# The prompt's up projection as seven half-size products (Strassen), with the sample's tokens as a plain pass in front

## The reference, cut to what matters

```
h = rmsnorm(x, norm2_g)
u = dwconv3(h @ w_up, ffn_conv_w, ffn_conv_b)     # w_up: 1024 x 5632; neighbours along the tokens
val, gate = u[..., :D_FF], u[..., D_FF:]           # D_FF = 2816
return x + (jax.nn.silu(gate) * val) @ w_down      # w_down: 2816 x 1024
```

## Time and profile before

| | |
|---|---|
| median of the runs | 2340.96 us (2334.17 to 2341.86) |
| span of the profiled execution | 2335.3 us |
| busy: PE, DVE, ACT, POOL | 2240.7, 1184.1, 782.4, 145.3 us |
| up projection, first to last matmul's start | 1238.3 to 1958.5 us |

### The profile page before, as it was taken

How to read it: one execution, slowest core, us unless ns; L and a number is a source line. 1 busy time by engine, 2 the same in 40 slices (tenths; PEclk the granted TensorE clock), 3 DMA queues, 4 the chain that set the end, 5 groups by cost and what they waited for, 6 DMA issues and landing times.

```text
span 2335.3 us, 26185 instructions
## 1 busy us (share of the span) xinstructions
PE 2240.7 (96%) x10340; PEld 1863.4 (80%) x10340; DVE 1184.1 (51%) x1655; ACT 782.4 (34%) x1193; POOL 145.3 (6%) x163
## 2 busy tenths in 40 slices
PE   6999999999998898877999999999999999999998
PEld 5788888888786787776888888888888887888886
DVE  6676776644833667766464334343333335324332
ACT  5432333345434444554253212121122213224221
POOL 0221122000110100100000000000000000000000
PEclk9999999999998999999999999999999999999999
DMA  4344444455556666777453111111111114435442
GB/s 146 113 146 138 124 143 147 136 160 167 184 182 184 179 211 187 225 196 245 142 180 109 56 62 64 59 63 54 64 60 68 50 45 142 147 113 180 153 153 86
DMA packets 213588, 307.23 MB, mean 132 GB/s; under 512 B 15480, under 2 KB 143864, under 8 KB 213466
## 3 DMA queue, kind: packets, MB, share of 16 engines
q1 hardware_dynamic: 200858, 256.00, 36.2%
q0 software_dynamic: 11312, 46.14, 5.4%
q10 hardware_dynamic: 1296, 3.41, 0.4%
HBM read 207.38 MB, written 72.16 MB: 120 GB/s over the span
## 4 chain that ended last, share of the span: by engine, by line
PE 51%; DMA 1%; DVE 1%; ACT 0%; issue 0%; DVEq 0%; POOL 0%; ACTq 0%; SPq 0%
PE mlp_acc L128 10%; PE mlp_acc L130 10%; PE mlp_acc L129 10%; PE mlp_dacc L128 7%; PE mlp_dacc L130 6%; PE mlp_dacc L129 6%; DMA out_s_raw<-y_scratch 1%; PE mlp_acc L2623 0%; DMA down_d_raw<-arg_w_down_t 0%; DVE down_d_lo L2565 0%; DMA g_scratch<-up_prod 0%; DMA down_s_raw<-g_scratch 0%; DVE out_s_lo L2521 0%; ACT out_s_hi L2439 0%; DVE up_prod L2560 0%
## 5 line engine op out<-in xcount | busy, mean ns | idle before, releaser
L128 PE MATMUL mlp_acc<-mlp_h_hi,up_w_hi 128*128 128x512 f32 x1056 | 411.1, 389 | 0.2 <-DVE mlp_h_lo L2543 0.2
L129 PE MATMUL mlp_acc<-mlp_h_lo,up_w_hi 128*128 128x512 f32 x1056 | 410.8, 389 | 0.0
L130 PE MATMUL mlp_acc<-mlp_h_hi,up_w_lo 128*128 128x512 f32 x1056 | 410.8, 389 | 0.0
L2548 DVE TENSOR_TENSOR up_w_lo<-up_w_raw,up_w_hi 128x1024 fp32r<-128x1024 f32 x44 | 53.8, 1225 | 388.2 <-ACT up_w_hi L2456 388.2
L128 PEld LDWEIGHTS mlp_acc<-mlp_h_hi,up_w_hi 128*128 128x128 f32 x1056 | 198.3, 188 | 41.6 <-DVE mlp_h_lo L2543 0.6
L130 PEld LDWEIGHTS mlp_acc<-mlp_h_hi,up_w_lo 128*128 128x128 f32 x1056 | 198.3, 188 | 41.1
L129 PEld LDWEIGHTS mlp_acc<-mlp_h_lo,up_w_hi 128*128 128x128 f32 x1056 | 198.3, 188 | 41.0
L128 PE MATMUL mlp_dacc<-down_d_hi,down_s_hi 128*128 128x512 f32 x528 | 206.2, 391 | 4.1 <-DVE down_d_lo L2565 2.6
L129 PE MATMUL mlp_dacc<-down_d_lo,down_s_hi 128*128 128x512 f32 x528 | 206.2, 390 | 0.0
L130 PE MATMUL mlp_dacc<-down_d_hi,down_s_lo 128*128 128x512 f32 x528 | 206.1, 390 | 0.0
L2456 ACT ACTIVATE up_w_hi<-up_w_raw 128x1024 fp32r<-128x1024 f32 x44 | 46.6, 1060 | 460.1 <-PE mlp_acc L130 460.1
(11 more groups left out here) (237 smaller groups left out, 3882.8 us busy)
## 6 DMA issues: line engine op xcount, KB each, us to landing
in_w_raw<-arg_w_in_t SPq DMA_DIRECT2D x58, 512.0 KB, 3.7
down_s_raw<-g_scratch SPq DMA_DIRECT2D x48, 512.0 KB, 4.4
up_w_raw<-arg_w_up_t SPq DMA_DIRECT2D x44, 512.0 KB, 3.5
g_scratch<-up_prod POOLq DMA_DIRECT2D x22, 768.0 KB, 3.5
filt_tab<-arg_fwd SPq DMA_DIRECT2D x32, 512.0 KB, 3.8
mix_classes<-mix_split SPq DMA_DIRECT2D x48, 256.0 KB, 8.9
mix_kf<-k_scratch SPq DMA_DIRECT2D x48, 256.0 KB, 3.4
mix_split<-mix_classes SPq DMA_DIRECT2D x48, 256.0 KB, 5.0
```

What stands on the lines that cost most here:

```text
L128: pe.matmul(out, w_hi, x_hi, start=first, stop=False)
L129: pe.matmul(out, w_hi, x_lo, start=False, stop=False)
L130: return pe.matmul(out, w_lo, x_hi, start=False, stop=last)
L2548: dve.tensor_tensor(w_lo[i % 2][:, :, :], raw[i % 2][:, :, :], w_hi[i % 2][:, :, :].bitcast(F32), ALU.subtract).then_inc(sem["w_low"], 1)
```

## The change

The up projection is now made in two passes.

**The sample first, plainly.** 44 tiles, each one chunk of 512 tokens (24 matmuls), into four rotating banks. `load_w`, `high_w`, `low_w`, `centre`, `gather`, `silu`, `gate` and `store` stay, for 512 tokens in place of 1536.

**Then the prompt by Strassen's algorithm** (Winograd's form). Its 1024 tokens are two halves of 512, the contraction two halves of 512, and the output channels of a pair two halves (value and gate). Four quarter operands b11, b12, b21, b22 of the activations and their sums t1 to t4 are made once: the new steps `turn_q` (four transposes of one quarter, line 2953), `copy_q`, `high_b`, `low_b`, `make_t`, `high_t`, `low_t`, four rounds `j` of them. For each pair `k` of weight tiles one load of 1024 KB (`load_a`) brings the weights again, four sums of weights are made on POOL (`sum`: four two-input operations of 128x512), and the groups a1, s23, s14 and a22 are split (`high_a`, `low_a`). Seven products of 4 x 3 = 12 matmuls each follow (`prod`), in the order p1, p6, p2, p7, p5, p4, p3, in three accumulator banks; a bank is read out in the middle and then accumulated into further (`evac`: s1, c11 on ACT; s2, s3, c22, c21, c12 on DVE). `centre_a`, `gather_a`, `silu_a`, `gate_a`, `store_a` are the convolution and the gate, for 1024 tokens, and now read the sums from SBUF (`c_sb`) in place of PSUM.

The down projection's token tiles are now taken with the sample's first (`down_at`), and its first weights and activations may be split as the last products release their memory (`d_free`).

```diff
-        if kind == "product":
-            i, c, _ = a
-            return "PE", 1.4, 0, [("low_w", i)] + ([("gather", i - 2)] if i >= 2 else [("low_x", TT - 1 if i else CH // P * (c + 1) - 1, 1)])
+        if kind == "product":
+            i = a[0]
+            return "PE", 1.4, 0, [("low_w", i)] + ([("gather", i - 4)] if i >= 4 else [("low_x", ns - 1, 1)])
...
+        if kind == "turn_q":
+            j = a[0]
+            return "PE", 0.5, 0, [("scale_x", ns + 2 * j + 1), ("low_t", j - 1, "t4") if j else ("scale_x", TT - 1)] + ([] if j else [last_out[2 * TT - 1], ("add_o", 1, TT - 1)])
...
+        if kind == "load_a":
+            k = a[0]
+            return "SP", 0.6, 6.0, ([("sum", k - 1, 3), ("low_a", k - 1, "a1"), ("low_a", k - 1, "a22")] if k else [("turn_q", across - 1, "b21")])
+        if kind == "sum":
+            k, n = a
+            return "POOL", 1.4, 0, [("load_a", k)] + ([("low_a", k - 1, "s14" if n in (0, 3) else "s23")] if k else [])
...
+        [("out", h, t, q) for h, t in rows_of for q in range(KD // 2)] + [("product", i, kq) for i in range(n_tiles) for kq in range(pieces)]
+        + [("prod", k, x) for k in ks for x in PRODUCTS],
+        [("turn_q", j, q) for j in js for q in ("b11", "b12", "b22", "b21")],
...
+                def load_a(k):
+                    if k:
+                        sp.wait_ge(sem["summed"], summed_per * k)
+                        sp.wait_ge(a_low["a1"], k)
+                        sp.wait_ge(a_low["a22"], k)
+                    else:
+                        sp.wait_ge(sem["turned_q"], 4 * across)
+                    sp.dma_start(raw_a[...], w_tiles[2 * k:2 * k + 2, :, :, :]...).then_inc(sem["raw_loaded_a"], 16)
...
+                        pool.wait_ge(sem["raw_loaded_a"], 16 * (k + 1))
+                        if k:
+                            pool.wait_ge(a_low["s14"], k)
+                        pool.tensor_tensor(s1, a21, a22, ALU.add).then_inc(sem["summed"], 1)
...
+                def turn_q(j, q):
+                    if (j, q) == (0, "b11"):
+                        pe.wait_ge(sem["xn_ready"], TT)
+                        pe.wait_ge(sem["added_o"], 2 * TT)
+                        pe.wait_ge(sem["low_x"], 2 * ns)
+                    elif q == "b11":
+                        pe.wait_ge(sem["low_q"], 7 * j)
+                    k, first = ns + 2 * j + (q in ("b12", "b22")), KH if q in ("b21", "b22") else 0
+                    for x in range(KH):
+                        c = first + x
+                        last = pe.transpose(q_bank[q][:, x, :], x_sb[:, k, c * P:(c + 1) * P], ident[:, :])
+                    last.then_inc(sem["turned_q"], 1)
+
+                def prod(k, x):
+                    q, at, other = OPERANDS[x]
+                    first = CHAINS[x][1]
+                    if (k, x) == (0, "p1"):
+                        pe.wait_ge(sem["low_q"], 7 * across)
+                        pe.wait_ge(sem["u_ready"], n_tiles)
+                    pe.wait_ge(a_low[q], k + 1)
+                    if not first:
+                        pe.wait_ge(sem[{"p2": "s1", "p7": "s2", "p4": "s3", "p3": "c22"}[x]], k + 1)
+                    elif k >= 2:
+                        pe.wait_ge(sem[{"p1": "c11", "p6": "c21", "p5": "c12"}[x]], k - 1)
+                    for kt in range(KH):
+                        last = three_pass(...)
+                    last.then_inc(done[x], 1)
```

More of the change, by code:

```diff
@@ new lines, in work @@
+        if kind == "load_a":
[4 more added lines that the diff above has]
+            return "POOL", 1.4, 0, [("load_a", k)] + ([("low_a", k - 1, "s14" if n in (0, 3) else "s23")] if k else [])
+        if kind == "high_a":
+            k, q = a
+            need = {"a1": [("load_a", k)], "a22": [("load_a", k)], "s23": [("sum", k, 2)], "s14": [("sum", k, 3)]}[q]
+            first = {"a1": [], "s23": [], "s14": [last_small], "a22": [("low_w", n_tiles - 1)]}[q]
+            return "ACT", 0.6 if q == "a22" else 1.1, 0, need + ([("prod", k - 1, GROUP_FREE[q])] if k else first)
@@ new lines, in work @@
+        if kind == "low_a":
+            return "DVE", 0.7 if a[1] == "a22" else 1.25, 0, [("high_a",) + a]
+        if kind == "prod":
+            k, x = a
+            need = [("low_a", k, OPERANDS[x][0])] + ([] if k else [("low_t", across - 1, "t4"), ("low_b", across - 1, "b21")])
+            if x in ("p1", "p6", "p5"):
+                need += [("evac", k - 2, {"p1": "c11", "p6": "c21", "p5": "c12"}[x])] if k >= 2 else [("gather", n_tiles - 1)]
+            else:
+                need += [("evac", k, {"p2": "s1", "p7": "s2", "p4": "s3", "p3": "c22"}[x])]
+            return "PE", 2.73, 0, need
@@ new lines, in work @@
+        if kind == "centre_a":
+            k, v = a
+            need = [("evac", k, "c21"), ("evac", k, "c22")] if v else [("evac", k, "c11"), ("evac", k, "c12")]
+            return "ACT", 1.1, 0, need + ([("store_a", k - 1) if v else ("gate_a", k - 1)] if k else [])
+        if kind == "gather_a":
+            return "DVE", 2.5, 0, [("centre_a",) + a]
+        if kind == "silu_a":
+            return "ACT", 1.1, 0, [("gather_a", a[0], 1)]
+        if kind == "gate_a":
+            return "DVE", 1.25, 0, [("silu_a", a[0]), ("gather_a", a[0], 0)]
```

454 lines of the change are left out of this document (340 added, 114 removed).

## The result

The changed kernel takes 2353.86 us in the median of ten runs (2343.24 to 2361.28); the kernel before, run beside it, 2337.8 in ten (2333.27 to 2341.86). The ratio is 1.0069, with a 95% interval of 1.0054 to 1.0085: the kernel became slower by 0.7%, where 2337 us had been forecast, about what the kernel before takes. The profiled executions have spans of 2335.3 and 2350.5 us. They are compared from here on, since they can be taken apart: +15.2 us, where the sum of the forecast was -3.9.

The account below looks back on a forecast made before the run. PE was taken to bound the kernel, each matmul worth 0.2267 us. -59.9 - 7.0 + 44 + 24 - 5 = -3.9 on the profiled 2335.3 us, its 5.7 below the median kept, gave 2337 us, range 2310 to 2365.

Parts of the forecast that it names:

- 264 products fewer: Up projection: 2904 matmuls in place of 3168, each worth 0.2267 us, -59.9 us.
- transposes leave the output stage and the first tiles: Ahead of the up projection: eight prompt tiles' transposes, 0.88 us each with a slower first matmul, go: -7.0 us.
- gap: Between the passes: PE idles through four uncovered transpose and split rounds and the first weights; p1 starts at S + 42.2.
- slow clock behind it: First prompt products: nine matmuls at half clock after the idle time between the passes, 1.7 us more.
- steady waits: Prompt's pass: POOL's sums hold DVE's neighbour additions, so p7 waits 1.2 us in 20 pairs: +24, bounds 0 and 40.
- start of down: Down projection's start: 5 of 6.0 us of waits and slow clock go, bounds -6 and -2.
- The step that made the load the last thing to be waited for: First pair: load waits for the last transpose, takes 4.8 us, lands at 38.0; splits and sums follow before p1.
- It fits with 0.2 us to spare: Prompt's pass: DVE's chain from p4 ends with s2 at 27.0 us, p7 is due at 27.2.
- rival (C): Prompt's pass: p7's wait is longer and TensorE's clock falls in it; at 2.2 us a pair 2391 us; chance 0.15.
- rival A: The forecast itself: idle time between passes and the sums meeting additions as costed, 2326 to 2354 us; chance 0.50.
- rival D: Between the passes: slow first load and late sums make it 52 in place of 44, 2345 us; chance 0.15.
- The base: Whole kernel: profiled 2335.3 us lies 5.7 below the median of 2340.96, a distance taken as unchanged.

Follow-up runs that it names:

- the transposes between the tiles: Changed kernel with the prompt quarters' transposes after every second sample tile from the ninth, splits beside the sample's: 2321.52 us (0.9943).
- sums made once: Changed kernel with POOL's four weight sums made for the first pair only and reused, output not the reference's: 2328.35 us (0.9954).
- sums late: Changed kernel with all work done, but POOL waits for s2 before the sums of the next pair but one: 2327.38 us (0.9954).
- the load later: Changed kernel with the load of the next pair but one issued behind the gate tile's centre step: 2353.79 us (1.0074).
- order and late sums: Changed kernel with c12 ahead of s14's low part, silu behind the value tile's centre step, POOL's sums behind s2: 2318.11 us (0.9915).
- the two kernels with all edits: Changed kernel with transposes between sample tiles, c12 and silu reordered, sums behind s2; with operands at multiples of 256 bytes 2278.05 us, without 2279.77.
- the first load early: Changed kernel with the first pair's weights loaded behind the first quarter round, sums and split still behind the last transposes: 2369.39 us, one run.
- both kernels with moved operands: Changed kernel with only the output projection's operands moved: split activations by 32 bytes, 2365.55 us (1.0113); operands at multiples of 256 bytes, 2348.65 (1.0048).

## Why the prediction came out as it did

In the profiled executions, in us:

| step | forecast | measured |
|---|---|---|
| 264 products fewer | -59.9 | -59.9 (2904 at 0.2267) |
| transposes leave the output stage and the first tiles | -7.0 | -7.0, but the output stage is only 2.6 and not 5.3 shorter (its matmuls cost 0.0067 more each): +2.6 |
| gap | +42.2 | +42.7 |
| slow clock behind it | +1.7 | +2.7 |
| steady waits | +24 | +30.0, and +3.2 slow clock, +1.6 slow first matmuls |
| start of down | -5 | -3.9 |
| stages ahead, end behind the last issue | 0 | +1.4, +1.9 |
| sum | -3.9 | +15.2 |

The measured rows add up to 15.3; the loose 0.1 is rounding. The measured 2354 us lie inside the stated range of 2310 to 2365, but its middle and the direction were missed: the sum said a little faster, and the kernel is slower, clear of the interval.

**The products** were right to the tenth, and so was what a matmul less is worth where nothing else ends last.

**The gap** was right, term by term: rounds 9.9 apart (forecast 9.9), the first load of 1024 KB 5.1 (4.8), p1 at S + 42.7 (42.2). The step on the clock was mis-sized: thirteen slow matmuls, not nine. That splitting without cover is the whole of the gap is shown by the transposes between the tiles. The step that made the load the last thing to be waited for is half wrong: taking it away gives nothing, because the sums that follow it run into DVE's own last round.

**The steady wait** is the step that failed: its term was +24, at 1.2 us a pair, and measured +34.8. These 10.8 us are over half of the 19.1 by which the sum was off, and by themselves they turn -3.9 into +6.9. The mechanism is as forecast, each link shown by a run or a trace: sums and two-SBUF additions exclude each other (sums made once: 2.19 back to 1.28), it is their meeting that costs and not their work (sums late), the waiting engine gets its turn between two instructions of the other, and the price follows the landing. The Trainium skill (page "SBUF — State Buffer", section "Who interferes with whom") says this of a VectorE instruction with two SBUF inputs, and that whoever is second is blocked; the traces agree with 2.19 for 1.28. Where the two starts lie within 0.05 us, though, it was the addition that stood, even when the trace has it first by 0.03 (2.40, and the sum 1.29). Two things were mis-sized. First, "It fits with 0.2 us to spare" was wrong: `centre_a` was taken from a copy's row, 1.06, and took 1.24 twice in the chain, so the chain is 0.43 late with no sum at all, and the usual wait is 1.34 above the normal distance and not 1.2. In the run without sums, the 0.63 between the two are 0.36 for the centre steps, 0.14 from the end of s2 to the start of p7, which the forecast left out, and 0.13 of handovers in the chain. Second, I took one price for all twenty pairs, though I had written that the price hangs on the landing, and had a rival (C) for the wait that is long enough for the clock to fall. In truth the two cases are mixed within one execution: sixteen usual, three long and one between in this one, eleven long in another. And the forecast had the price rise with a later landing; that a landing 0.1 us earlier costs 1.1 us, through the second sum, it did not have. The sum needs the price times its share for both, 30.0 + 3.2, and 1.6 for the first matmul behind each wait, which takes 0.31 to the next start.

The range of rival A was also added up too narrow: 0.8 and 1.9 us a pair with the gap's bounds of 39 and 50 make 2324 to 2357 and not 2326 to 2354, and rival D's gap of 52 lies outside these bounds. Neither changes the forecast.

**The output stage** was costed as only shorter. That the new layout of the tiles puts the split operands elsewhere in SBUF, and that the place has a price, I did not look for; 576 matmuls at 0.0067 are 3.9; a wait of 0.8 that the stage had before is gone, and half a microsecond of the difference stays without a name.

**The start of down** fell by 3.9 of the 5 within its bounds. **Ahead and behind:** the stages before the output projection are the same in both kernels, and the first matmul of that projection lies anywhere between 1093.2 and 1100.5 in the traces here, so +1.4 says nothing. The 1.9 behind the last store's issue are in all the kernels with the change; what they are was not tried.

**The base.** 5.7 us lie between the span and the median of the three runs shown; the later ten and more runs put the kernel before at 2336.8 to 2338.1, and a run's time is 1.7 to 1.8 above its span. That moved the forecast up by some 3 us, so its total (2337 for 2353.9) was less far off than its sum, which is luck.

Why it is slower then, in one line: gains of 71 us (59.9, 7.0 and 3.9) stand against 45 for the gap with its slow clock, 35 for the steady waits and 6 of small terms; the forecast had the waits 11 us too low and the other terms, each by 0.5 to 3 us and all to the same side, some 8 us too low together.

## What to carry to other kernels

A saving of PE time is worth what the new uncovered work leaves of it; look first for other work that the new step can stand beside, since the same splits, put between the sample's tiles, cost 9 us and not 45. Before two-input work is put on POOL, list which DVE instructions with two SBUF operands can meet it and who waits behind those; a wait on a semaphore that moves the meeting to where nobody waits was worth 26 us here, and together with an order that shortens DVE's chain 36. Where a chain fits by less than a microsecond, price each link by its own shape and operation, and expect more than one outcome within a single execution.

## What the runs showed of the hardware

- The matmul's pace depends on where its operands start in SBUF. The places are counted from the stage's first operand by the sizes in the source, since no trace has addresses. With the weights' side (`out_s_hi` and the second `out_s_lo`) at 32 bytes beyond a multiple of 256 and the moving side (`out_w_hi`, `out_w_lo`) at 128 beyond one the distance is 0.2334; with the weights' side moved to 64 beyond, 0.2309; with all of them at multiples of 256, 0.2268, as in the kernel before, where they also stood so. So the weights' side counts. Which side gave the last 0.0041, when both moved (and `out_s_raw`, which TensorE does not read, with them), was not separated.
- TensorE's clock behind a wait is not a matter of its length alone. In two executions of the changed kernel PE waits 2.1 us at the same place where the down projection starts. In the first it kept the full clock (stretch 1989 to 1991), in the second eight matmuls ran at the lower of the two levels, 1.2 GHz, for 1.6 us more in the stage (1998 to 2000):

```profile
1989.00:1991.00 2.00, 1.84 (x8) 1.52 (x9) 2.00 (x3) 0.87 (x1) 0.00 (x0) 1.00 0.99 373
```

```profile
1998.00:2000.00 2.00, 2.00 (x6) 1.61 (x7) 2.00 (x2) 0.76 (x2) 0.00 (x0) 0.64 1.01 383
```

- In twenty waits of up to 1.8 us idle (the load later) it never fell; in the changed kernel, behind 2.03 and 2.23 it did, behind 2.28 it did not. In front of the down projection it fell behind 1.93 (order and late sums), and of the two kernels with all edits behind 1.94 in one and not in the other.
- Sums on POOL and additions on DVE, both with two SBUF operands, have a sharp edge. In the six traces with the sums and the load where the change has them (the changed kernel twice, the transposes between the tiles, the first load early, and both kernels with moved operands), 25 value tiles had the second sum start between 0.09 us ahead of the first addition and 0.05 behind it, and all 25 additions took 2.28 to 2.42. Wherever it started from 0.05 to 0.35 us behind, the addition took its 1.28 or 1.29 and the sum stood.
